# A two-network block in one kernel: the modulation's product in plain 32-bit matmuls, and GpSimd's subtraction in halves

## The reference

```python
silu_c = jax.nn.silu(c)                     # (1, 1024)
silu_cc = jax.nn.silu(c_ctx)                # (1024,)
mod = (silu_c @ w_ada[l] + b_ada[l])[:, None, :]
sh1, sc1, g1, sh2, sc2, g2 = jnp.split(mod, 6, axis=-1)
mod_c = jnp.split(silu_cc @ w_ada[l][:, :n_cm * D_MODEL] + ..., n_cm)
```

## Time and profile before

| | us |
|---|---|
| median of 3 runs | 3389.98 (3389.87 to 3398.14) |
| the profiled execution | 3398.09 |
| its span (first to last instruction) | 3396.2 |
| PE / DVE / ACT / POOL busy | 2967.0 / 2264.4 / 1629.2 / 2448.3 |
| mean granted TensorE clock | 0.93 of full |
| DMA | 441.64 MB, mean 130 GB/s |

### The profile page before, as it was taken

One profiled execution on the slowest core, in us unless ns is written; L12 is line 12 of the kernel. 1 busy time (PEld: TensorE's weight loads), 2 busy tenths in 40 slices (PEclk: granted clock), 3 DMA queues, 4 the chain that ended last, 5 costly groups with the idle time before them and its releaser, 6 DMA issues.

```text
span 3396.2 us, 59887 instructions
## 1 busy us (share of the span) xinstructions
PE 2967.0 (87%) x21332; PEld 2725.6 (80%) x21332; DVE 2264.4 (67%) x2987; ACT 1629.2 (48%) x3327; POOL 2448.3 (72%) x2290
## 2 busy tenths in 40 slices
PE   6988868899889888889988888878899989998998
PEld 4887757799889766779987887767799869996898
DVE  3994785676797478577643974795666466646665
ACT  4545335454545524545545545234454545555454
POOL 6996677878799757767865997536778627874687
PEclk7999978999989988999998998888999989998999
DMA  5433333445433323334542433313445314542354
GB/s 193 149 118 100 106 124 125 137 153 171 137 121 128 124 87 118 125 118 146 177 136 75 137 121 114 100 58 106 165 162 179 118 50 149 177 156 77 125 175 165
DMA packets 121578, 441.64 MB, mean 130 GB/s; under 512 B 13552, under 2 KB 15600, under 8 KB 120992
## 3 DMA queue, kind: packets, MB, share of 16 engines
q1 hardware_dynamic: 121088, 435.30, 38.7%
q10 hardware_dynamic: 288, 3.47, 0.3%
HBM read 437.67 MB, written 1.05 MB: 129 GB/s over the span
## 4 chain that ended last, share of the span: by engine, by line
POOL 47%; issue 36%; PE 11%; DVE 4%; ACT 1%; POOLq 1%; DMA 0%; DVEq 0%; SPq 0%; ACTq 0%
POOL w_lo L1004 47%; PE lin L464 3%; PE lin L465 3%; PE lin L466 3%; DVE arena L1701 2%; POOLq L1006 1%; ACT w_hi L1035 1%; POOLq L1002 0%; PE aux L636 0%; PE aux L596 0%; DVE s_lo L1639 0%; DMA w_raw<-in_stream 0%; ACT arena L1197 0%; PE lin L728 0%; DVE rstd L1576 0%
## 5 line engine op out<-in xcount | busy, mean ns | idle before, releaser
L1004 POOL TENSOR_TENSOR w_lo<-w_raw,w_hi 128x256 fp32r<-128x256 f32 (+1 forms) x2286 | 2448.1, 1101 | 941.5 <-ACT w_hi L1035 938.1
L464 PE MATMUL lin<-h_hi,w_hi 128*128 128x256 f32 x3584 | 1039.1, 290 | 56.9 <-POOL w_lo L1004 33.2
L1035 ACT ACTIVATE w_hi<-w_raw 128x512 fp32r<-128x512 f32 x1638 | 937.8, 623 | 240.4 <-PE lin L464 107.9
L465 PE MATMUL lin<-h_lo,w_hi 128*128 128x256 f32 x3584 | 1023.2, 285 | 0.0
L466 PE MATMUL lin<-h_hi,w_lo 128*128 128x256 f32 x3584 | 1022.3, 285 | 0.0
L464 PEld LDWEIGHTS lin<-h_hi,w_hi 128*128 128x128 f32 x3584 | 697.0, 194 | 76.3 <-issue 42.6
L465 PEld LDWEIGHTS lin<-h_lo,w_hi 128*128 128x128 f32 x3584 | 697.0, 194 | 0.4
L466 PEld LDWEIGHTS lin<-h_hi,w_lo 128*128 128x128 f32 x3584 | 696.6, 194 | 0.0
L1701 DVE SCALAR_TENSOR_TENSOR arena<-arena,vec 128x256 f32<-128x256 f32 x720 | 497.0, 761 | 0.1
L464 PE MATMUL lin<-s_hi,w_hi 128*128 128x256 f32 x1392 | 415.8, 299 | 32.5 <-DVE s_lo L1639 27.7
L465 PE MATMUL lin<-s_lo,w_hi 128*128 128x256 f32 x1392 | 403.5, 290 | 0.0
(11 more groups left out here) (254 smaller groups left out, 4526.5 us busy)
## 6 DMA issues: line engine op xcount, KB each, us to landing
w_raw<-in_stream SPq DMA_DIRECT2D x819, 512.0 KB, 3.3
X<-in_tokens SPq DMA_DIRECT2D x2, 1024.0 KB, 10.7
arena<-in_const ACTq DMA_DIRECT2D x1, 1856.0 KB, 9.0
arena<-in_small ACTq DMA_DIRECT2D x1, 1536.0 KB, 13.5
out<-arena SPq DMA_DIRECT2D x1, 1024.0 KB, 3.9
arena<-in_masks SPq DMA_DIRECT2D x1, 960.0 KB, 12.0
const<-in_const SPq DMA_DIRECT2D x1, 690.0 KB, 7.6
wglr<-in_w_glr SPq DMA_DIRECT2D x1, 384.0 KB, 9.8
```

What stands on the lines that cost most here:

```text
L464: used(pe.matmul(o, whi, hi[:, k, :], start=k == 0, stop=False), first)
L465: pe.matmul(o, whi, lo[:, k, :], start=False, stop=False)
L1004: ins = pool.tensor_tensor(w_lo[:, slot, part], w_raw[:, slot, part], w_hi[:, slot, part].bitcast(F32), ALU.subtract)
L1035: act.activation(w_hi[:, slot, part], w_raw[:, slot, part], ACT.Copy).then_inc(sems["hi_ready"], 1)
```

## The change

The modulation's product leaves the stream. Its weights become a tensor of their own (`ada`, 96 chunks of 128 output columns, 512 KB each, in the order of use). A unit is now one chunk: eight plain 32-bit matmuls with the weight as the stationary operand and the two vectors (2 columns) streaming, straight into the layout that is wanted. There is no split, no return (`ada_back`, `returned`, "pair", c_hl and mod_rows go), and one ACT copy per unit. The first 16 chunks have places in memory that is free at the start, and SP issues their DMAs ahead of the three stream loads. The other 80 go through one buffer (a_raw): ACT issues the next chunk's DMA right behind the copy of the unit before. The units are spread anew (14, 12 and 14 in the level stages; 8, 12 and 4 in attention; 3 beside the context pass's heads; 4 at its output product; 3 in each norm stage). DVE adds the bias for as many neighbouring chunks as it can in one instruction. The stream shrinks by 96 loads. Apart from this, PIECES goes from 4 to 2: outside the feed-forward POOL subtracts in two halves of 512 columns.

```diff
-PIECES = 4
+PIECES = 2
+ADA_CHUNKS = 6 * D // P
+ADA_FIRST = 2 * D // P
...
+def ada_units(l, s, stage):
+    counts = {(0, CTX): (14, 3, 8, 4, 3), (0, LAT): (12, 0, 12, 0, 3), (1, LAT): (14, 0, 4, 0, 3)}[l, s]
+    first = ADA_FIRST if s == CTX else 27 if l else 0
+    at = first + sum(counts[:stage])
+    return [("ada", (max(l, s), c)) for c in range(at, at + counts[stage])]
...
+        a_raw = sb("a_raw", [P, KC, P])
...
+            for c in range(ADA_FIRST):
+                sp.dma_start(a_first[c], ada_in[c]).then_inc(first_landed[c // 4], 16)
             for s in range(SLOTS):
                 sp.dma_start(w_raw[:, s, :], stream[s]).then_inc(landed[s], 16)
...
-                    whi, wlo, first = weight(ADA_CHUNKS)
-                    used(pe.matmul(o[0:4, 0:ADA_COLS], c_hl[:, k, :], whi, start=k == 0, stop=False), first)
-                    mm = pe.matmul(o[0:4, 0:ADA_COLS], c_hl[:, k, :], wlo, start=False, stop=k == KC - 1)
+                if k0 < ADA_FIRST:
+                    w = a_first[k0]
+                    if k0 % 4 == 0:
+                        pe.wait_ge(first_landed[k0 // 4], 4 * 16)
+                else:
+                    w = a_raw
+                    pe.wait_ge(sems["ada_landed"], 16 * (k0 - ADA_FIRST + 1))
+                o = bank()
+                for k in range(KC):
+                    mm = pe.matmul(o[:, 0:2], w[:, k, :], cvec[:, k, :], start=k == 0, stop=k == KC - 1)
                 done(mm)
...
+            def ada(l, c):
+                moved(act.activation(mod[:, l, c, :], arrived(0)[:, 0:2], ACT.Copy))
+                ada_moved.append((l, c))
+                following = len(ada_moved) - ADA_FIRST
+                if 0 < following < len(ADA_LATER):
+                    act.dma_start(a_raw[:, :, :], ada_in[ADA_FIRST + following]).then_inc(sems["ada_landed"], 16)
...
+            act.activation(cvec[:, :, :], cvec[:, :, :], ACT.Silu).then_inc(sems["c_ready"], 1)
+            act.dma_start(a_raw[:, :, :], ada_in[ADA_FIRST]).then_inc(sems["ada_landed"], 16)
             split_to(SLOTS)
```

More of the change, by code:

```diff
@@ L113, in spread, with woven, key_fill @@
     return [[u for k, u in enumerate(units) if k * steps // len(units) == j] for j in range(steps)]
[L116 to L128, removed]
+def ada_units(l, s, stage):
[3 more added lines that the diff above has]
+    return [("ada", (max(l, s), c)) for c in range(at, at + counts[stage])]
+GLA_STAGE, HEAD_STAGE, ATT_STAGE, OUT_STAGE, NORM_STAGE = range(5)
+def woven(a, b):
+    n = max(len(a), len(b))
+    return [u for k in range(n) for x in (a, b) for u in x[k * len(x) // n:(k + 1) * len(x) // n]]
+FIRST_UNITS = [("ada", (0, c)) for c in range(ADA_FIRST)]
 def head_fill():
     return {2: ("go", 1), 4: ("go", 2), 6: ("go", 3), 8: ("go", 4)}
+def key_fill(l, s):
+    return dict(zip((0, 2, 4), ada_units(l, s, HEAD_STAGE)))
 def attention_fill(l, s):
[L138 to L141, removed]
+    return woven([("go", c) for c in range(5, KC)] + [("gc", c) for c in range(KC)], ada_units(l, s, ATT_STAGE))
 def gla_fill(l, s):
[L146 to L149, removed]
+    return woven([(kind, c) for c in range(KC) for kind in ("r", "gg")], ada_units(l, s, GLA_STAGE))
 def out_fill(l, s):
[L154 to L157, removed]
+    return dict(zip((1, 2, 4, 5), ada_units(l, s, OUT_STAGE)))
 def norm_fill(l, s):
-    return [("ada", (max(l, s), g)) for g in ((22, 23) if s == CTX or l else (10, 11))]
+    return ada_units(l, s, NORM_STAGE)
 STEPS = 2 * len(LEVELS) + 1
@@ L497, in token_major, with ada @@
                             done(mm)
-            rows = {}
-            def ada(group):
+            ada_done = {}
+            def ada(unit):
+                k0 = len(ada_done)
+                ada_done[unit] = k0
+                if k0 < ADA_FIRST:
[5 more added lines that the diff above has]
+                    pe.wait_ge(sems["ada_landed"], 16 * (k0 - ADA_FIRST + 1))
                 o = bank()
                 for k in range(KC):
-                    whi, wlo, first = weight(ADA_CHUNKS)
-                    used(pe.matmul(o[0:4, 0:ADA_COLS], c_hl[:, k, :], whi, start=k == 0, stop=False), first)
-                    mm = pe.matmul(o[0:4, 0:ADA_COLS], c_hl[:, k, :], wlo, start=False, stop=k == KC - 1)
[L508 to L518, removed]
+                    mm = pe.matmul(o[:, 0:2], w[:, k, :], cvec[:, k, :], start=k == 0, stop=k == KC - 1)
                 done(mm)
@@ L1988, in _ @@
                     gla(l, s)
[L1990 removed]
+                    n.up("lin_evac", KVH)
+                    for c in range(HEADS):
+                        n.up("lin_evac")
+                        if c in key_fill(l, s):
+                            unit(l, key_fill(l, s)[c])
+                    n.up("lin_evac", QT)
                     inverse(aux[0], ROWS, name="row_ready")
@@ L2177, in paired, with ada_tiles @@
     return np.stack([tiles(a), tiles(b)], 1)
-def wide_tiles(w):
-    return [token_tiles(w[:, g * ADA_COLS:(g + 1) * ADA_COLS]) for g in range(ADA_GROUPS)]
+def ada_tiles(layers):
+    both = [tiles(w["w_ada"]).reshape(ADA_CHUNKS, KC, P, P).transpose(0, 2, 1, 3) for w in layers]
+    return np.stack([both[l][c] for _, (l, c) in FIRST_UNITS + ADA_LATER])
 def half_tiles(gate, up, down):
@@ L2204, in unit @@
         def unit(kind, c):
-            return none[0] if kind == "adt" else ada[c[0]][c[1]] if kind == "ada" else chunks[kind][c]
+            return none[0] if kind == "ada" else chunks[kind][c]
         for s in (CTX, LAT):
@@ L2214, in first_stack_tiles @@
             parts += [paired(g_att, w["w_att_o"]), tiles(w["w_conv_o"])]
-            beside = out_fill(l, s)
-            for c, chunk in enumerate(tiles(w["w_out"])):
-                parts += [chunk, unit(*beside[c]) if c in beside else none[0]]
-            parts += [unit(*u) for u in norm_fill(l, s)]
+            parts += [tiles(w["w_out"])]
             parts += half_tiles(w["w_ff_gate"], w["w_ff_up"], w["w_ff_down"])
```

94 lines of the change are left out of this document (40 added, 54 removed).

## The result

The changed kernel takes 3400.65 us (median of 20 runs, 3391.82 to 3410.03) against 3391.09 us for the kernel before (20 runs beside them, 3385.51 to 3400.34): a ratio of 1.0022, 95% interval 1.0012 to 1.0032. That is within the 0.3% named as no change; the forecast of 3269 us, and the whole range 3200 to 3345, missed it. The profiled executions stand at 3390.0 us of span against 3396.2.

A forecast was written before the change was run, and what follows sets the result against it. POOL was taken to set the pace beside a busy DVE, with PE waiting for w_lo. The terms -2 - 8 - 52 - 48 - 8 - 6 - 2 + 5 gave -121 us from 3390, so 3269 us; range 3200 to 3345 for 8 in 10.

The forecast's parts named there:

- Added: 96 units at 0.9 us: Each new unit's eight plain 32-bit matmuls take PE 0.11 us apiece, 86 us against 120 us for the removed group products.
- First stage: 0 to 73.2 us: squares wait for the stream loads, units run at half clock in 28 us; ends at 71 to 72, -2.
- Input stages: Three stages of 32 loads without groups: halves save some 8 us where POOL was late; -8, bounds -36 and +35.
- Level stages: Gated attention: fewer POOL pieces relieve DVE by 0.48 us each; 12 us once and 20 twice, -52, bounds -25 and -80.
- Attention: Three passes: first -28, second -22, third +2 from fewer POOL pieces; sum -48, bounds -25 and -75.
- natural experiment: Earlier trace: third-pass attention without groups took 107.6 us, second 130.2 with the same DVE instructions; 0.40 us per piece.
- Heads, output product, norms: POOL-paced output product -8, three norm stages -6, rest including the heads stage -2.
- One buffer: ACT issues the single buffer's next DMA behind a copy; mostly hidden, some PE waits, +5, bounds 0 and +150.
- The rival that put 150 us on it: The buffer's round trip sets the pace at 66 of 80 units, 2.3 us each: +152, 3416 us; slower 0.06.
- Halves hold DVE: DVE's vector chains wait 1.28 us behind a half instead of 0.70: +70, 3340 us; 0.16 shared with PE alone.
- PE was never held by POOL: Only PE's own 34 us go, giving 3356 us; chance 0.16 shared with halves holding DVE.
- More relief: Each removed piece gives DVE its full 0.70 us, first stage at full clock, buffer free: -182, 3208 us; 0.15.

The follow-up runs named there:

- e3: The changed kernel with each modulation unit multiplying only four of its eight 128-row parts; 0.9885 of the kernel before, 39 us under it.
- e2: The changed kernel with GpSimd's subtraction back in four pieces (quarters); 0.8% faster than the changed kernel, 0.9944 of the kernel before.
- e5: The changed kernel with each modulation unit multiplying only one of its eight parts; 3.0% (101 us) faster than the changed kernel.
- e1: The kernel before with only GpSimd's subtraction outside the feed-forward changed, to two halves instead of four pieces; 1.3% (44 us) slower than the kernel before.
- e8: Stream loads first, plus two useless plain 32-bit matmuls of 256 columns ahead of each of the 16 first units; 0.6% slower than e4.
- e4: The changed kernel with SyncE issuing the three stream loads ahead of the first units' 16 weights; 0.3% (10 us) faster than the changed kernel.

## Why the prediction was wrong, point by point

The forecast was -121 us; by the ratio the kernel is 7 us slower, and the profiled spans differ by -6.2. By its own steps (differences of the profiled stages):

- **Added: 96 units at 0.9 us. This step failed.** The price per record was right, the count was half. A unit is 1.84 us. In the level stages this is 40 units x 0.94 = 38 us more on PE, and halving the units' matmuls (e3) takes 23.4 us off these stages. "Bounds 0.11 and 0.22" was written per matmul; a bound that includes the count of records would have been 0.22 to 0.44, and with it the swap on PE changes sign. The count is not the whole miss: against the changed kernel, e3 at the forecast's price brings 46 us, quarters in place of halves (e2) 26, of some 128 missed. The two were not run together, and the remaining 56 us or so are only in part placed below.
- **First stage, -2, measured +24.2.** The queue was followed rightly: squares forecast at 38, measured 37.76; first unit 41, measured 43.5. The units were to take 28 us and took 50.2: the double count again, less what the first 5 us at full clock gave back. That all of it would run at half clock was nearly right, and not for the reason given: the clock was back at full when the units began and fell while PE was 100% busy with them.
- **Input stages, -8, measured +13.1.** The pairs were reckoned from 1.28 and 1.46 us for a half; the mean of all 786 is 1.486, the shut-outs in it. The bounds -36 and +35 held it. I had hoped that halves would be rid of the stuck piece in the second stage, and left room for more of them only in the upper bound; one came in every input stage, of 19.7 us each. e2 shows -10.8 without halves.
- **Level stages, -52, measured -12.2.** At the forecast's price of a unit e3 has -35.6, within the bounds -25 and -80: 23 of the missed 40 us are the PE term above, the other 16 are relief that was put too high. Only with two records a unit (e5) is it -48.5.
- **Attention, -48, measured -57.2.** Right, a little small: the first 28.9 less (forecast 28), the second 28.4 less (22), the third 0.1 more (2). The natural experiment in the earlier trace rows was the best ground in the whole working (the third pass's attention, which had no group to lose, kept its length).
- **Heads, output product, norms, -16, measured +30.0.** Two causes: for halves alone e1 has +22.6 on heads and output product, and e5, with its cheap units, +21.1, so the units' full price adds only 9 to that (+30.3), and at half of the product (e3, +29.3) it is not less at all. With quarters (e2) the heads come back to +2.3, but the output product keeps +12.1, against the -8 that I had booked for it by calling one window POOL-paced (58.4 of 62.9 us busy); what holds it there is open. The heads stood in a rest of -2.
- **One buffer, +5.** Right in kind: PE's matmuls wait for a_raw's DMA 7.6 us in all (its loads 9.3), and the landing is 3.4 us. The rival that put 150 us on it is refuted by these waits.
- **The marks named for a wrong forecast.** I had named over 0.15 us per plain matmul at full clock; it is 0.21 to 0.23. "Input stages longer by over 10 us each" didn't come (+9.0, +1.5, +2.6). Loads are 723 as forecast, and PE waits for no w_lo ahead of a unit.

Of the rivals, "Halves hold DVE" named a mechanism that the runs show beside the count: halves cost 44 us on the kernel before and 26 on the changed one, the shut-outs of GpSimd included, where I gave DVE's waits alone +70. It didn't come alone, and no rival joined it with a dearer unit. "PE was never held by POOL" is refuted by the attentions, 55 to 57 us shorter with a PE that has no less to do in e2 and the changed kernel. "More relief" is refuted: even with an eighth of the matmuls (e5) the attentions gain 55 us and not the 88 that 0.70 us for each of 125 pieces would make.

The Trainium skill, "SBUF — State Buffer", whose rule of the exclusive lock I weighed and set aside for the 0.88 us pair, also says, in section "SBUF: two separate sides", that the engine that starts first has the ports for the whole instruction and the other is blocked for as long. For the heads the trace fits that part: halving the number of pieces and doubling their length cost DVE 7.0 us. That a GpSimd instruction can be kept out for 19.7 us, over some 45 DVE instructions in a row, goes beyond one instruction. Nor is it the halves' length alone: quarters were kept out for 11.7 us too.

## What to carry to other kernels

Count what one instruction of the program becomes in the trace before pricing a new one from its nearest row: records divided by program matmuls, on a line that already has that type. When one engine is relieved, sum up the next one's busy time stage by stage after the change; where it comes out near the stage's length (here PE in the level stages), the relief ends there. And the size of GpSimd's pieces is chosen per stage: here short pieces paid where DVE works through a chain, long ones where PE sets the pace. When the failed step is found, build the kernel that has it at the forecast's price (here e3): what it still misses was another step's fault.

## What the runs showed of the hardware

- A plain 32-bit matmul with 128 x 128 weights and 2 columns is two records, which follow each other every 0.11 us at full clock (16 in 1.84 us, or in 1.70 to the next matmul's start) and every 0.21 at half: nearly as much as two fp32r matmuls of 256 columns (0.121 each in the feed-forward).
- PE at 100% busy with these matmuls had a granted clock of 0.50 (1.2 GHz) from 50 to 90 us in the first stage, and also with 256-column matmuls as 4 of each 20 records (e8, 40 to 80 us). The clock didn't only fail to rise: it was full when the units began, and fell to half (at 48 us in the changed kernel, at 26 us in e4 and e8) while PE was 100% busy. In the level stages, with units among the dense products, it is 0.96 to 0.99.
- GpSimd's subtraction was shut out for 6.0 to 20.1 us beside a row of DVE steps with two tensor inputs at 0.40 us each, and let in when DVE paused for its own last step. With halves the row of 50 steps then took 40.91 us where it had taken 19.87.
